# Delta core of a gated DeltaNet: first inverse by VectorE's 32-block transposition, R added on VectorE, decayed values scaled on ScalarE

## The reference, cut to what matters

```python
L = jnp.where(strict, jnp.einsum('bhncd,bhnsd->bhncs', kb, k) * decay, 0.0)
rhs = jnp.concatenate([v * beta[..., None], kb * jnp.exp(g)[..., None]], axis=-1)
sol = lax.linalg.triangular_solve(eye + L, rhs, left_side=True, lower=True, unit_diagonal=True)
u, w = sol[..., :DV], sol[..., DV:]
qk = jnp.where(tril, jnp.einsum('bhncd,bhnsd->bhncs', q, k) * decay, 0.0)
...
def step(S, xs):
    qk_i, u_i, w_i, qd_i, kd_i, gl_i = xs
    v_new = u_i - jnp.einsum('bhcd,bhde->bhce', w_i, S)
    o = jnp.einsum('bhcd,bhde->bhce', qd_i, S) + jnp.einsum('bhcs,bhse->bhce', qk_i, v_new)
    S = S * gl_i[..., None, None] + jnp.einsum('bhcd,bhce->bhde', kd_i, v_new)
    return S, o
```

## Time and profile before

| | |
|---|---|
| median of 3 runs | 4576.62 us (4575.06 to 4580.44) |
| profiled execution: time | 4570.06 us |
| profiled execution: span, first to last instruction | 4568.1 us |
| busy share of the span | PE 90%, PEld 75%, DVE 51%, ACT 50%, POOL 44% |
| mean granted TensorE clock, as a share of 2.4 GHz | 0.948 |

### The profile page before, as it was taken

One profiled execution on the slowest core, in us unless ns is written; L12 is line 12 of the kernel. 1 busy time (PEld: TensorE's weight loads), 2 busy tenths in 40 slices (PEclk: granted clock), 3 DMA queues, 4 the chain that ended last, 5 costly groups with the idle time before them and its releaser, 6 DMA issues. The chain is left out here.

```text
span 4568.1 us, 83170 instructions
## 1 busy us (share of the span) xinstructions
PE 4101.5 (90%) x30756; PEld 3422.6 (75%) x30756; DVE 2332.6 (51%) x2947; ACT 2279.5 (50%) x4473; POOL 2017.4 (44%) x1524
## 2 busy tenths in 40 slices
PE   6689999999999969999999999986999599978779
PEld 2367777777777758888888888875888488856657
DVE  3234433444434446666666666655554423238853
ACT  4335555555654636666666666652111511148832
POOL 2245555555545546677777777743111412100022
PEclk8789999999999989999999999998999599988889
DMA  6245544445445456676667666654443322354245
GB/s 229 86 126 149 150 141 143 146 145 149 143 144 149 145 177 198 198 200 197 198 197 199 196 200 197 200 166 172 175 178 138 97 105 113 126 204 188 82 136 138
DMA packets 775798, 733.24 MB, mean 161 GB/s; under 512 B 111808, under 2 KB 702656, under 8 KB 758272
## 3 DMA queue, kind: packets, MB, share of 16 engines
q1 hardware_dynamic: 775456, 728.67, 51.3%
HBM read 483.12 MB, written 245.33 MB: 159 GB/s over the span
## 5 line engine op out<-in xcount | busy, mean ns | idle before, releaser
L565 PE MATMUL pj_bank<-h_hi,pj_whi 128*128 128x512 f32 (+1 forms) x1920 | 724.6, 377 | 21.0 <-POOL pj_wlo L551 20.8
L565 PE MATMUL pj_bank<-h_lo,pj_whi 128*128 128x512 f32 (+1 forms) x1920 | 711.7, 371 | 0.0
L565 PE MATMUL pj_bank<-h_hi,pj_wlo 128*128 128x512 f32 (+1 forms) x1920 | 710.0, 370 | 0.0
L751 POOL TENSOR_TENSOR pj_BD<-pj_E,pj_gi 128x512 f32<-128x512 f32 x144 | 194.6, 1352 | 650.4 <-ACT pj_E L888 650.4
L1354 ACT ACTIVATE dc_R<-dc_psE 128x256 f16<-128x256 f32 x864 | 285.0, 381 | 371.4 <-PE dc_psE L1231 371.3
L1428 DVE TENSOR_TENSOR dc_Y<-dc_psY,dc_pick 128x256 f16<-128x256 f32 x864 | 325.1, 417 | 277.7 <-PE dc_psY L1217 277.7
L565 PEld LDWEIGHTS pj_bank<-h_hi,pj_whi 128*128 128x128 f32 x1920 | 366.8, 191 | 88.9 <-POOL pj_wlo L551 21.3
L565 PEld LDWEIGHTS pj_bank<-h_lo,pj_whi 128*128 128x128 f32 x1920 | 365.9, 191 | 64.9 <-issue 5.7
L565 PEld LDWEIGHTS pj_bank<-h_hi,pj_wlo 128*128 128x128 f32 x1920 | 365.1, 190 | 62.0
L933 DVE RECIPROCAL pj_acc<-pj_acc 128x2304 f32<-128x2304 f32 x16 | 232.8, 14553 | 260.8 <-ACT pj_acc L865 260.8
L1146 POOL TENSOR_TENSOR dc_A<-dc_Lhi,dc_id 128x512 f16<-128x512 f16 x144 | 166.3, 1155 | 416.0 <-ACT dc_Lhi L1345 416.0
(11 more groups left out here) (267 smaller groups left out, 10394.3 us busy)
## 6 DMA issues: line engine op xcount, KB each, us to landing
dc_dd<-scratch_decays SPq DMA_DIRECT2D x288, 256.0 KB, 5.5
dc_tm<-scratch_tm SPq DMA_DIRECT2D x288, 192.0 KB, 2.5
pj_E<-scratch_cgrow SPq DMA_DIRECT2D x288, 128.0 KB, 3.7
scratch_decays<-pj_E SPq DMA_DIRECT2D x144, 256.0 KB, 3.8
scratch_decays<-pj_BD SPq DMA_DIRECT2D x144, 256.0 KB, 3.7
dc_fm<-scratch_fm SPq DMA_DIRECT2D x288, 128.0 KB, 3.3
dc_egr<-scratch_egrow SPq DMA_DIRECT2D x288, 128.0 KB, 3.7
scratch_o<-dc_ob SPq DMA_DIRECT2D x288, 128.0 KB, 3.1
```

The costliest lines, as they stand in the source:

```text
L565: i = pe.matmul(self.bank[blk][:, 0:n], l[b][:, k, :], r[:, k, at:at + n], start=(m == 0), stop=(m == 3 * KT - 1))
L751: pool.tensor_tensor(BD[b][:], E[b][:], gi[b][:, :, Q_BETA, :].unsqueeze(3).broadcast_to(C4), ALU.mult).then_inc(s["d_scaled"], 1)
```

## The change

R's first value is made by one VectorE instruction that transposes 32 by 32 blocks of X in SBUF (X is non-zero only in 2 by 2 blocks on the diagonal). `newton_r` no longer adds R on TensorE; VectorE's new `last` adds R to the correction while it evicts it. The correction of p = 0 goes to the bank psV (shared with `solved`), that of p = 1 to the bank psE of p = 1. VectorE does `last` of p = 1 at the end of a step and `last` of p = 0 in the next step, after `level(1)` and before `right_side` of p = 0. The Newton part takes p = 1 first. `faded_v` moves to ScalarE, as four instructions of 128 x 128 with the decay as a per-partition scale, ahead of `new_v`, which no longer waits for it. VectorE's `first` stands after `state` at l = 5 and 6.

```diff
...
         bG, bZ, bV, bO = (bank(x) for x in "GZVO")
+        newton_bank = (bV, bE[1])
         par = lambda x: [sem(f"dc_{x}{p}") for p in range(2)]
...
             par("s_" + x) for x in ("vb", "xr", "vs", "vn", "Sd", "S", "ob", "out"))
-        s_const, s_id = sem("dc_const"), sem("dc_idle")
+        s_Rf, s_const, s_id = par("s_Rf"), sem("dc_const"), sem("dc_idle")
         flat = lambda t: t[:].rearrange("p d h t -> p (d h t)")
...
                     m.then_inc(p_gram[p], 1)
-                def first(j, q, p):
-
-                    pe.wait_ge(s_x0[p], j + 1)
-                    wait(pe, eY[p], j * LV)
-                    for c in range(4):
-                        m = pe.matmul(comb(bY[p], c), comb(X[q][p], c), id16[:, 0:P], start=True, stop=True)
-                    m.then_inc(pY[p], 1)
-
                 def level_y(j, q, l, p):
...
                         pe.wait_ge(eF[p], j + 1)
+                        wait(pe, eY[p], j * LV)
                     else:
-                        pe.wait_ge(eR[p], j * U + l - 1)
+                        pe.wait_ge(eR[p], j * LV + l - 1)
                     for c in range(4):
...
                     if l == 1:
-                        wait(pe, eR[p], j * U)
                         wait(pe, eX[p], j * U)
+                        if p == 1:
+                            wait(pe, s_Rf[1], j)
                     else:
...
                 def newton_e(j, q, p):
-                    pe.wait_ge(eR[p], j * U + LV)
+                    pe.wait_ge(eR[p], j * LV + LV)
                     pe.wait_ge(eX[p], j * U + LV)
...
                 def newton_r(j, q, p):
                     pe.wait_ge(eX[p], j * U + U)
-                    pe.matmul(flat(bE[p]), id16[:, 0:P], flat(R[q][p]), start=True, stop=False)
+                    if p == 0:
+                        wait(pe, s_vs[1], j)
+                        wait(pe, s_vn[1], j)
                     for c in range(4):
-                        m = pe.matmul(comb(bE[p], c), comb(X[q][p], c), comb(YN[p], c), start=False, stop=(c == 3))
+                        m = pe.matmul(comb(newton_bank[p], c), comb(X[q][p], c), comb(YN[p], c), start=True, stop=True)
                     m.then_inc(pR[p], 1)
                 def state_by_k(i, q, p):
...
                 def solved(i, p):
                     pe.wait_ge(s_xr[p], i + 1)
-                    pe.wait_ge(eR[p], (i + 1) * U)
+                    pe.wait_ge(s_Rf[p], i + 1)
                     wait(pe, s_vn[1 - p], i + p)
...
                         beside_rx(l)
-                    if make:
-                        for p in range(2):
-                            first(i + 2, q, p)
                     if inv:
-                        for p in range(2):
+                        for p in (1, 0):
                             newton_e(j, 1 - q, p)
...
                     if inv:
-                        for p in range(2):
+                        for p in (1, 0):
                             newton_r(j, 1 - q, p)
...
                     act.activation(Lhi[p][:], L32[p][:], ACT.Copy).then_inc(s_lhi[p], 1)
-                def first(j, q, p):
-                    act.wait_ge(pY[p], j * U + 1)
-                    wait(act, pR[p], j - 1)
-                    act.activation(R[q][p][:], bY[p][:], ACT.Copy).then_inc(eF[p], 1)
-
                 def level_r(j, q, l, p):
...
                     act.activation(all_cols(X[q][p], l, False), split4(quart(bE[p], 1), l), ACT.Copy).then_inc(eX[p], 1)
-                def last(j, p):
-                    act.wait_ge(pR[p], j + 1)
-                    wait(act, p_v[p], j)
-                    act.activation(Rf[p][:], bE[p][:], ACT.Copy).then_inc(eR[p], 1)
+                def faded_v(i, q, p):
+                    g = gr[q][p]
+                    act.wait_ge(p_v[p], i + 1)
+                    wait(act, p_up[p], i)
+                    for c in range(4):
+                        m = act.activation(comb(vs[p], c), comb(bV, c), ACT.Copy, scale=g[:, c // 2, Q_ELG, c % 2:c % 2 + 1])
+                    m.then_inc(s_vs[p], 1)
                 def new_v(i, p):
                     act.wait_ge(p_v[p], i + 1)
-                    act.wait_ge(s_vs[p], i + 1)
                     wait(act, p_out[p], i)
...
                         if rec and l in (3, 5):
+                            faded_v(i, q, l // 2 - 1)
                             new_v(i, l // 2 - 1)
-                    if make:
-                        for p in range(2):
-                            first(i + 2, q, p)
                     if rec:
                         outputs(i, 1)
-                    if inv:
-                        for p in range(2):
-                            last(j, p)
                 run(act)
...
                 def level(j, l, p):
-                    dve.wait_ge(pY[p], j * U + 1 + l)
+                    dve.wait_ge(pY[p], j * LV + l)
                     dve.tensor_tensor(all_cols(Y[l - 1][p], l, True), split4(quart(bY[p]), l),
...
                     m.then_inc(s_xr[p], 1)
-                def faded_v(i, q, p):
-                    dve.wait_ge(p_v[p], i + 1)
-                    wait(dve, p_up[p], i)
-                    dve.tensor_tensor(vs[p][:], bV[:], tok(gr[q][p], Q_ELG), ALU.mult).then_inc(s_vs[p], 1)
+                def first(j, q, p):
+                    dve.wait_ge(s_x0[p], j + 1)
+                    wait(dve, pR[p], j - 1)
+                    wait(dve, s_Rf[p], j - 1)
+                    dve.transpose(flat(R[q][p]), flat(X[q][p])).then_inc(eF[p], 1)
+                def last(j, q, p):
+                    dve.wait_ge(pR[p], j + 1)
+                    wait(dve, p_v[p], j)
+                    dve.tensor_tensor(Rf[p][:], newton_bank[p][:], R[q][p][:], ALU.add).then_inc(s_Rf[p], 1)
                 def state(i, q, p):
...
                                 level(j, l, p)
+                        if rec and l == 1:
+                            last(i, q, 0)
                         if rec and l in (1, 3):
...
                             scores(i + 2, q, (r + 2) % 4, l // 2 - 1)
-                        if rec and l in (3, 5):
-                            faded_v(i, q, l // 2 - 1)
                         if rec and l in (5, 6):
                             state(i, q, l - 5)
+                        if make and l in (5, 6):
+                            first(i + 2, q, l - 5)
                     if inv:
-                        for p in range(2):
+                        for p in (1, 0):
                             newton(j, p)
+                        last(j, 1 - q, 1)
                 run(dve)
```

## The result

| | before | changed |
|---|---|---|
| median | 4575.84 us (4 runs, 4560.26 to 4580.44) | 4714.54 us (4 runs, 4709.38 to 4721.64) |
| profiled execution, span | 4568.1 us | 4712.5 us |
| mean granted clock, share of 2.4 GHz | 0.948 | 0.946 |
| busy, PE / DVE / ACT | 90% / 51% / 50% | 87% / 51% / 48% |

The ratio is 1.031, 95% interval 1.0293 to 1.0328. A second set of five runs of the changed kernel gave 1.0321 (1.0302 to 1.0339). From the start of the core's first group of matmuls to the start of its last 1530.9 us pass (1672.16 to 3203.02) where it was 1379.2 (1678.55 to 3057.74): +151.7. The rest of the program differs by -7 us in these two profiled executions; over all the runs profiled here it lies between 3180 and 3210 us, so its differences say nothing about the change.

A forecast was written before the change was run, and what follows sets the result against it. TensorE's ordered list and operands late for its head set the step. Delays 1.18 + 1.08 + 0.26 + 0.23, less 0.88 removed, gave +1.87 us x 72 = +135 on 4576.6: 4712 us, range 4655 to 4765.

The forecast's parts named there:

- the likeliest case: The forecast itself, whole program: 4712 us, +1.87 us a step, given a chance of 0.62.
- TensorE work removed: TensorE's list: transposing products (0.45 us) and identity products of `newton_r` (0.43) go, -0.88 us a step.
- F: ScalarE: time from the start of the first of four scaled copies to the last one's end, taken as 1.20 us.
- The delays of `update`: TensorE's `update` waits for ScalarE's decayed values: F - 0.02 = 1.18 us for p = 0, F - 0.12 = 1.08 for p = 1.
- X of level 6: TensorE's `newton_e` waits for X of level 6, p = 1, the last of ScalarE's four copies: +0.26 us a step.
- `last` ahead of `right_side`: VectorE's `last` of p = 0 delays `right_side`, so `state_by_k` of p = 1 waits: +0.23 us a step.
- t: The start of the next step on TensorE, from which VectorE's `last`, `level(1)` and `right_side` are timed.
- The transposition costs nothing: VectorE's transposition hides before its next due work: 0 us; rival of a dear one, 4790 to 4960 us, chance 0.07.
- The covers of 1.37 and 1.54 us: VectorE time from the transposition's start to its next due work: 1.37 us for p = 0, 1.54 for p = 1.
- The clock: Rival: TensorE's granted clock falls to 1.2 GHz for a tenth of the work, 1.8 us a step, about 4840; chance 0.04.
- The sum: Whole step: (F - 0.02) + (F - 0.12) + 0.26 + 0.23 - 0.88 = +1.87 us, x 72 = +135 us.
- either small wait: TensorE's waits before `newton_e` for X and before `state_by_k` of p = 1 for xr, forecast at 0.2 to 0.3 us.

The follow-up runs named there:

- experiment 1: The changed kernel with the decayed values back on VectorE in one pass of 128 x 512: 4539.7 us, ratio 0.9925 to the kernel before.
- experiment 6: The changed kernel with copies ahead of `level_r`, `level_x` of level 6 taking p = 1 first, and `last` of p = 0 behind `right_side`: 4493.1 us, ratio 0.9817.
- experiment 2: The kernel before with only the decayed values moved to ScalarE, as four scaled copies ahead of `new_v`: 4766.2 us, ratio 1.0414.
- experiment 3: The changed kernel with the four scaled copies ahead of `level_r` at l = 3 and 5 instead of behind `level_x`: 4536.9 us, ratio 0.9906.
- experiment 7: The changed kernel with one scaled copy of 128 x 512 instead of four, leaving out three combinations' decays: 4641.0 us, ratio 1.0138.
- experiment 4: The changed kernel with `level_x` of level 6 taking p = 1 first: 4686.9 us, ratio 1.0246 to the kernel before.
- experiment 5: The changed kernel with VectorE's `last` of p = 0 behind `right_side` of p = 0: 4694.8 us, ratio 1.0262 to the kernel before.
- experiment 8: The changed kernel with each transposition done twice, the extra one into an unread tile: 4725.5 us, ratio 1.0318 to the kernel before.
- experiment 9: The changed kernel with each transposition done three times, the two extra ones into unread tiles: 4728.9 us, ratio 1.0335 to the kernel before.

## Why the prediction came out right

4712 us was forecast, 4714.5 measured, in the range and by the likeliest case. By its steps:

- **TensorE work removed**, -0.88: right; in the trace `newton_r` is 0.44 us shorter and the transposing group of 0.45 is gone, and experiments 1 and 6 close their sums with it to 0.01 us. No run takes the products out alone.
- **F**, 1.20 taken, 1.17 measured. Its parts were less good than their sum: one copy takes 405 ns, not 371, and the copies start 250 ns apart, so that neighbours overlap by 0.15 us, not 0.10; the two errors cancel. The delays of `update`, forecast 1.18 and 1.08, are 1.16 and 1.06. Experiments 1, 2, 3 and 7 show that these two are the loss. By the Trainium skill's figures (ScalarE: Activation LUTs, section What ACT_TABLE_LOAD costs) F was an estimated 1.27, 0.1 us too high; its 93 ns for the operand lie between what the single copy of experiment 7 shows against the earlier trace rows, 0.71 us where 0.595 stand without the operand, and against `new_v` in its own trace, 0.63.
- **X of level 6**: forecast 0.26, measured 0.30; shown by experiment 4.
- **`last` ahead of `right_side`**: forecast 0.23, measured 0.26; shown by experiment 5. Here too two small errors offset each other: `right_side` starts at t + 1.85, not 1.90, and `state_by_k` follows its end by 0.14 us, not by 0.05.
- **The transposition costs nothing**: right, 0.70 us, shown by experiments 8 and 9. The covers of 1.37 and 1.54 us were too small, since I counted to VectorE's next due work and not to the one who waits for that.
- **The clock**: this was a rival with 0.04, at a tenth of all work, with "these waits are 1 us each" against it, and a clock of 1.00 was among the signs to look for. It did fall, in 10 of 71 steps, 1.61 us each, 16 us. The sum had left it out. Sum by the trace: 72 x 1.90 + 16 = 153 us in the core, where 151.7 passed; less the 7 us by which the rest of the program was shorter in that execution. So the central value was nearer than its working deserved, by luck: 16 us of clock were missing, and the difference of the medians, 138.7 us, is 13 below the core's growth, within the spread of the rest of the program.

What stays open: why the fall comes in every seventh step and not in all, when each has the same waits. It isn't chance: the second set's trace and those of experiments 8 and 9, with the same step of 20.74, have it 146.8 us apart too, and experiment 2, with a step of 21.06, has it 64.8 us apart in 20 of 22 cases. The runs show besides that 0.3 us less of either small wait all but ends it (9 or 10 slow steps to 1 and 0), that 0.46 less of each large one ends it (experiment 7), and that experiment 2, with the same large waits and without the two small ones, has more than twice as many (23). So the length of the waits alone doesn't tell.

## What to carry to other kernels

Where one engine's hand-written list is without gaps, as here, moving work off it pays its length, and moving work elsewhere costs what it makes the head of that list wait, however idle the other engine is on average. So look for the idle time at the place: the same four copies cost 2.2 us a step behind `level_x` and nothing ahead of `level_r`. When a list gets new neighbours, check the order of the parities on both sides of each hand-over: p = 1 first on TensorE wants p = 1 first on ScalarE.

## What the runs showed of the hardware

- Granted clock: in a step of 20.74 us with waits of TensorE of 1.29 and 0.89 us beside smaller ones it fell to 1.2 GHz in every seventh step (10 of 71), 1.61 us lost each time; with 0.3 us less of waits a step there was one such step (experiment 4) and none (experiment 5).
- VectorE's transposition of 128 x 512 in fp16 takes 701 ns alone, about the 0.68 us of a pass that reads PSUM, and three in a row take 1.9 us. The Trainium skill (VectorE: DVE Perf Modes, section The three transpose paths) gives 311 ns for 128 x 128 in bf16; four times that, an estimated 1.24 us, is well above the one instruction measured here.
- ScalarE's copies with a per-partition scale: 1.17 us for four of 128 columns from PSUM (405 ns each, starting 250 ns apart), 0.71 for one of 512.
